# Two residual norms moved behind the products that follow them, and first projections started on six of eight feature tiles

## The chip, the cores and the metric

The kernel runs on one core of one Trainium2 chip. The metric is the device time of one execution in microseconds (us). The core has five engines that run side by side and meet only through semaphores: TensorE (PE, matrix products and transposes), VectorE (DVE), ScalarE (ACT), GpSimd (POOL) and SyncE (SP, which here only starts the weight DMAs).

## The reference, cut to what matters

256 tokens with 1024 features run through one first block and two layers of a second model; all is float32. The change touches the second half of the first block:

```python
merged = gate_a * (ya @ w_proj_a[i]) + gate_b * (yb @ w_proj_b[i])
h = h + merged @ w_out[i]
h = h + memory_cross_attention(rms_norm(h, xattn_norm_g[i]), memn, w_q[i], w_k[i], w_v[i], w_xo[i])
h = h + swiglu(rms_norm(h, ffn_norm_g[i]), w_gate[i], w_up[i], w_down[i])
# rms_norm(x, g) = x * rsqrt(mean(x * x) + 1e-6) * g, one factor per token
# swiglu(n) = (silu(n @ w_gate) * (n @ w_up)) @ w_down
# attention: softmax(q k^T / 16) v, 4 heads of 256, 256 memory rows
```

Each of the two later layers has the form `merged @ w_out` too, followed by a layer norm. The last layer ends in a mixture of experts, which fills the second half of the run.

## The kernel before

**Tiles.** The residual `h` lies in SBUF with tokens on partitions, as two blocks of 128 tokens by 1024 features. A product needs its input with features on partitions, so normed values are transposed by TensorE against an identity (8 feature tiles of 128, called k 0 to 7). PSUM has 8 banks of 128 x 512. Work is cut into units, one bank each, in the order of `plan_units`; a unit's bank is its number modulo 8.

**Split products.** The large products work on pairs of fp32r tiles: a value is its fp32r copy ("high", made by ACT) plus the rest ("low", made by DVE as value minus high). One product is then three matmuls: high x high, high x low, low x high. A weight chunk (1 MB, 256 output columns for 8 feature tiles) is thus 48 matmuls of 256 columns: `split_b` with tokens as output partitions, `split_a` with features as output partitions.

**Weights.** SP streams chunks into a ring of 7 slots (L556 to L563). ACT makes the high copy (`wp_part`, L1386), DVE the rest (`wp_rest`, L1841), into two slots wp 0 and 1; chunk n may be copied only when the unit that used chunk n-2 is full. The FFN has three slots of its own (`wf_part` L1363, `wf_rest` L1860).

**Order of work around the change.** Every engine's program is an order written out by hand:
- PE waits for all four quarters of `merged` (`m_split`, L1013), makes units out 0 to 2 (one quarter of 256 features of the residual each) and then the last quarter as two half units `last_out` 0 and 1, one per token block.
- DVE adds each unit to `h` (`residual`, L1767). For each half unit `last_norm` (L1890) adds it, finishes the statistics, waits for ACT's square root, takes the reciprocal and writes the normed block `xn` (L1900).
- PE transposes a normed block as soon as it stands (`block_transposes`, L657); ACT copies the transposed values times the norm's gain to `xf_h` (L1402), DVE writes `xf_l` (L1880). When all of it stands, the four q units (L713) run.
- Attention over memory follows (4 heads), then units xo 0 to 2 and `last_xo` in the same manner as out, then the first block's FFN: 11 steps of gate (48 matmuls, L832), up (48) and down (24 of 512 columns, L845).
- Layers 0 and 1 start their own out product with the same wait for four quarters (L1089).

The square root lives in another activation table than exp and silu, so ACT loads it beforehand (`load_sqrt`, L1276).

Of the kernel before, what the change touches and what calls it, by code (L numbers as in the profile page):

```python
# [31 lines left out]
P = 128  # L32
# [105 lines left out]
def split_plan():  # L138

    out = [((("k8", "w_" + n, i)), (n, i) if n == "q" or i < 3 else ("last_" + n, TB - 1))  # L140
           for n in ("out", "q", "xo") for i in range(4)]
# [12 lines left out]
def plan_units():  # L154
# [25 lines left out]
    add("out", 3)  # L180
    add("last_out", TB)
    add("t_xattn", 4)
    add("q", 4)
    attention_units(u, "x", 4)
    add("xo", 3)
    add("last_xo", TB)
    add("t_ffn", 4)
# [14 lines left out]
    return u  # L202

# [47 lines left out]
def build(nc, a, out):  # L251
    with ExitStack() as ctx:
# [27 lines left out]
        rsum = sb("rsum", [P, 2, 2 * TB])  # L280
        esink = sb("esink", [P, 2, 2 * TB])
# [96 lines left out]

        z_t = view(big, 8192, 2048, "p (b d) -> p b d", b=TB)
# [35 lines left out]
        block_ready = sem("block_ready")  # L415
# [211 lines left out]
        def _(pe):  # L627
# [77 lines left out]
            def split_a(unit, chunk, tiles=(0, 1)):  # L705
# [4 lines left out]
                for j in tiles:  # L710
                    for k in range(KD):
                        for i, (w, x) in enumerate(((wh, xf_h), (wh, xf_l), (wl, xf_h))):
# [7 lines left out]
            def split_b_block(unit, chunk, b, at):  # L720

                wh, wl = split_chunk(chunk)
                for k in range(KD):
                    for i, (x, w) in enumerate(((xf_h, wh), (xf_h, wl), (xf_l, wh))):
# [14 lines left out]
            def last_split_b(name, chunk):  # L739

                for b in range(TB):
                    open_unit(pe, (name, b))
                    close_unit(split_b_block((name, b), chunk, b, 0), (name, b))
# [133 lines left out]
            def ffn(name, next_unit):  # L877
                f0 = ff0[name]
                all_banks_free(next_unit)
                for n, (part, s) in enumerate(FF_ORDER):  # L880
                    if part == "gate" and s >= 2:
# [131 lines left out]
            pe.wait_ge(m_split, 4)  # L1013
# [4 lines left out]
            for b in range(TB):  # L1018
# [10 lines left out]
            for i in range(3):  # L1029
                split_b(("xo", i), ("k8", "w_xo", i))  # L1030
            last_split_b("last_xo", ("k8", "w_xo", 3))
            for b in range(TB):
                pe.wait_ge(block_ready, TB + b + 1)
                block_transposes("t_ffn", xn, b)
            evacuated(pe, ("t_ffn", 3))
            ffn("ffn", UNIT_AT[("t_in0", 0)])

            for m in range(2):
# [50 lines left out]
                pe.wait_ge(m_split, 4 + 4 * (m + 1))  # L1089
                for i in range(3):  # L1090
# [168 lines left out]
        def _(act):  # L1259
# [47 lines left out]
            def attention(name, heads, dst_of):  # L1307
                g0 = head0[name]
                for i in range(heads + 2):
                    if i < heads:  # L1310
                        g = g0 + i
                        act.wait_ge(negm_ready, g + 1)
                        for b in range(TB):
                            last = nc.scalar.activation(prob[:, g % 2, b, :],
                                                        bank((name + "_s", i))[:, b * 256:(b + 1) * 256], ACT.Exp,
                                                        bias=negm[:, g % 2, b:b + 1], scale=XSCALE,
# [78 lines left out]
            def copy_xf_gain(u0, b, gain):  # L1395

                for half in range(2):
                    u = (u0, 2 * b + half)
                    take_unit(act, u)
                    for j in range(4):  # L1400
                        k = 4 * half + j
                        last = nc.scalar.activation(xf_h[:, k, b * P:(b + 1) * P], bank(u)[:, j * P:(j + 1) * P],  # L1402
                                                    ACT.Identity, scale=gains[:, gain, k:k + 1])
                    last.then_inc(xf_high, 1)
# [7 lines left out]
            def ffn(name):  # L1412
                f0 = ff0[name]
                for n, (part, s) in enumerate(FF_ORDER):
                    if part == "gate":
                        act.wait_ge(g_full, f0 + s + 1)
                        if s >= 1:
                            act.wait_ge(hT_ready, f0 + s)
                        nc.scalar.activation(silu[:, :], psum[:, ff_bank(name, 2 * (s % 2)), :],
                                             ACT.Silu).then_inc(silu_ready, 1)  # L1420
# [98 lines left out]
            for _ in range(3):  # L1519
                wp_part()  # L1520
            load_sqrt()
            for b in range(TB):
                std_block(b)
            for b in range(TB):
                copy_xf_gain("t_xattn", b, 2)
            wp_part()
            for i in range(4):
                if i < 3:
                    wp_part()
                out_of(("q", i), qT[:, 2 * i:2 * i + 2, :], ACT.Copy)  # L1530
            attention("x", 4, lambda i: xf_h[:, 2 * i:2 * i + 2, :])
            for _ in range(3):
                wp_part()
            for n in range(SPLITS - 1):
                wf_part("ffn", n)
            load_sqrt()
            for b in range(TB):
                std_block(b)
            for b in range(TB):
                copy_xf_gain("t_ffn", b, 3)  # L1540
            wf_part("ffn", SPLITS - 1)
            ffn("ffn")
# [141 lines left out]
        def _(dve):  # L1684
# [11 lines left out]
            def stats(src, rms, eps, meanwhile=None):  # L1696
# [3 lines left out]
                for b in range(TB):  # L1700
                    for c in range(2):
# [71 lines left out]
            def attention(name, heads):  # L1773
                g0 = head0[name]
                for i in range(heads + 2):
                    if i < heads:
# [4 lines left out]
                        V.tensor_scalar(negm[:, g % 2, 0:TB], mx[:, g % 2, 0:TB], -XSCALE, None,  # L1781
# [12 lines left out]
                    if i >= 2:  # L1794
                        xf_rest_of((name + "_o", i - 2), "x_o", i - 2)
# [53 lines left out]
            def xf_rest_of(unit, use, i):  # L1849
# [3 lines left out]
                high = xf_h[:, 2 * i:2 * i + 2, :].bitcast(F32)  # L1853
                free_unit(V.tensor_tensor(xf_l[:, 2 * i:2 * i + 2, :], halves(bank(unit)), high, ALU.subtract), unit)
# [16 lines left out]
            def xf_rest_gain(u0, b, gain):  # L1871

                for half in range(2):
                    u = (u0, 2 * b + half)
                    take_unit(dve, u)
                    dve.wait_ge(xf_high, 4 * XF_USES.index(u0) + 2 * b + half + 1)
                    for j in range(4):
                        k = 4 * half + j
                        at = slice(b * P, (b + 1) * P)
                        last = V.scalar_tensor_tensor(xf_l[:, k, at], bank(u)[:, j * P:(j + 1) * P],  # L1880
                                                      gains[:, gain, k:k + 1], xf_h[:, k, at].bitcast(F32),
                                                      ALU.mult, ALU.subtract)
                    free_unit(last, u)

            def first_half_stats():

                for b in range(TB):
                    V.bn_stats(st[:, b, 0, :], h[:, b, 0:512])

            def last_norm(name, u0, gain):  # L1890

                for b in range(TB):
                    u = (name, b)
                    take_unit(dve, u)
                    hs = h[:, b, 768:1024]
                    free_unit(V.tensor_tensor(hs, hs, bank(u)[:, 0:256], ALU.add), u)
                    evacuated(dve, u)
                    block_stats(h, b, True, EPS, (1,))
                    block_rstd(b)
                    V.tensor_scalar(xn[:, b, :], h[:, b, :], rstd[:, b:b + 1], None, ALU.mult).then_inc(block_ready, 1)  # L1900
                for b in range(TB):
                    xf_rest_gain(u0, b, gain)

            def ffn(name):
                f0 = ff0[name]
                for n, (part, s) in enumerate(FF_ORDER):
                    if part == "up":
# [13 lines left out]
            def add_sums(name, n, b, alpha=None):  # L1921

                dve.wait_ge(down_done, FF_STEPS * n - (TB - 1) + b)
                for c in range(2):
                    hs = h[:, b, c * 512:(c + 1) * 512]
                    acc = psum[:, acc_bank(name, b, c), :]
                    if alpha is None:
                        last = V.tensor_tensor(hs, hs, acc, ALU.add)
# [192 lines left out]
            for i in range(3):  # L2121
                if i < 2:
                    wp_rest()
                residual(("out", i), i)
                if i == 1:
                    evacuated(dve, ("out", 1))
                    first_half_stats()
            wp_rest()
            evacuated(dve, ("out", 2))
            last_norm("last_out", "t_xattn", 2)  # L2130
            for _ in range(4):
# [385 lines left out]
```

## Time and profile before

| | |
|---|---|
| times of three runs | 2264.4, 2268.22, 2270.58 us (median 2268.22) |
| profiled execution | 2270.2 us, span of its records 2268.4 us |
| PE busy | 2144.6 us, 95% |
| DVE, ACT busy | 1577.0 us (70%), 1196.4 us (53%) |
| mean granted TensorE clock | 0.971 of 2.4 GHz |

The span is the time from the first to the last instruction. Lines such as L725 are lines of the kernel before; a line can be a helper's that several stages share, so stages are told apart by time. The out product runs from 296 to 321 us, q from 330 to 355, attention to 384, xo to 411, and the first FFN from 420 to 602 us.

### The profile page before, as it was taken

What the parts mean: (1) busy time and instruction counts of PE and PEld (TensorE: products, weight loads), DVE (VectorE), ACT (ScalarE), POOL (GpSimd) and SP (SyncE); (2) the same over time, 40 slices, a digit from 0 to 9 for tenths busy, and PEclk for the clock granted to TensorE, in tenths of its full rate; (3) what the DMA queues carried; (4) which work ended last, traced back from release to release, by engine and by line L of the source; (5) the groups of instructions that cost most, each with busy time, mean ns of one, the idle gap of its engine ahead of it and who ended that gap; (6) DMA issues with size and microseconds to landing.
All of it is one profiled execution on the core that took longest, in us unless ns stands there. A gap on an engine that the chain in (4) does not pass through costs nothing.

```text
span 2268.4 us, 33197 instructions
## 1 busy us (share of the span) xinstructions
PE 2144.6 (95%) x12590; PEld 1876.3 (83%) x12590; DVE 1577.0 (70%) x1775; ACT 1196.4 (53%) x1233; POOL 9.8 (0%) x22
## 2 busy tenths in 40 slices
PE   7999988899898989998888999999999999999997
PEld 7888877899797779998877788888888888888885
DVE  8677353544636454454555888989898989899897
ACT  3300233433337433343552677777777777777774
POOL 0000000000000000000000000000000000000000
PEclk9999998899999989999998899999999999999998
DMA  7343332355463235555323798989898989989894
GB/s 300 138 151 112 145 121 87 136 186 185 160 244 109 97 138 185 186 197 192 142 78 129 276 371 344 364 350 367 339 366 342 365 352 361 371 337 370 349 357 162
DMA packets 76446, 542.02 MB, mean 239 GB/s; under 512 B 9152, under 2 KB 9296, under 8 KB 11968
## 3 DMA queue, kind: packets, MB, share of 16 engines
q1 hardware_dynamic: 72144, 524.32, 60.3%
q0 software_dynamic: 2080, 10.40, 1.2%
q10 hardware_dynamic: 2128, 5.93, 0.7%
q8 instruction: 73, 1.20, 0.2%
q14 instruction: 21, 0.17, 0.0%
HBM read 539.57 MB, written 1.05 MB: 238 GB/s over the span
## 4 chain that ended last, share of the span: by engine, by line
PE 88%; DVE 6%; ACT 4%; issue 2%; DMA 0%; DVEq 0%; ACTq 0%
PE psum L1192 13%; PE psum L832 11%; PE psum L1169 9%; PE psum L1173 9%; PE psum L1172 9%; PE psum L666 7%; PE psum L713 6%; PE psum L725 6%; PE psum L845 4%; PE psum L679 3%; PE psum L692 3%; PE psum L1135 2%; PE psum L1181 1%; ACT wp_h L1386 1%; PE psum L989 1%
## 5 line engine op out<-in xcount | busy, mean ns | idle before, releaser
L2247 DVE TENSOR_TENSOR w_l<-ring,w_h 128x2048 fp32r<-128x2048 f32 x338 | 773.5, 2291 | 116.1 <-ACT w_h L1372 109.4
L1372 ACT ACTIVATE w_h<-ring 128x2048 fp32r<-128x2048 f32 x338 | 647.5, 1916 | 140.4 <-PE psum L1169 96.8
L1169 PE MATMUL psum<-w_h,xe_h 128*128 128x512 f32 x896 | 359.9, 402 | 2.4 <-DVE xe_l L2331 2.4
L1173 PE MATMUL psum<-w_h,xe_l 128*128 128x512 f32 x896 | 350.8, 391 | 0.0
L1172 PE MATMUL psum<-w_l,xe_h 128*128 128x512 f32 x896 | 350.2, 391 | 0.0
L1860 DVE TENSOR_TENSOR wf_l<-ring,wf_h 128x2048 fp32r<-128x2048 f32 x66 | 151.2, 2291 | 156.2 <-ACT wf_h L1363 156.2
L1841 DVE TENSOR_TENSOR wp_l<-ring,wp_h 128x2048 fp32r<-128x2048 f32 x52 | 119.1, 2292 | 163.5 <-ACT wp_h L1386 163.5
L832 PE MATMUL psum<-xf_h,wf_h 128*128 128x256 f32 x704 | 201.6, 286 | 4.7 <-DVE xf_l L1880 3.0
L832 PE MATMUL psum<-xf_l,wf_h 128*128 128x256 f32 x704 | 201.3, 286 | 0.0
L832 PE MATMUL psum<-xf_h,wf_l 128*128 128x256 f32 x704 | 201.3, 286 | 0.0
L1169 PEld LDWEIGHTS psum<-w_h,xe_h 128*128 128x128 f32 x896 | 168.8, 188 | 38.3 <-DVE w_l L2247 4.0
L1173 PEld LDWEIGHTS psum<-w_h,xe_l 128*128 128x128 f32 x896 | 168.6, 188 | 36.1
L1172 PEld LDWEIGHTS psum<-w_l,xe_h 128*128 128x128 f32 x896 | 169.1, 189 | 32.3
L1363 ACT ACTIVATE wf_h<-ring 128x2048 fp32r<-128x2048 f32 x66 | 126.0, 1912 | 114.0 <-PE psum L845 58.5
L1386 ACT ACTIVATE wp_h<-ring 128x2048 fp32r<-128x2048 f32 x52 | 99.5, 1916 | 141.4 <-PE psum L725 72.8
L832 PEld LDWEIGHTS psum<-xf_h,wf_h 128*128 128x128 f32 x704 | 137.5, 195 | 6.2 <-DVE xf_l L1880 3.4
L1192 PE MATMUL psum<-w_h,eT_h 128*128 128x512 f32 x448 | 140.0, 394 | 0.0
L1192 PE MATMUL psum<-w_h,eT_l 128*128 128x512 f32 x448 | 138.4, 390 | 0.0
L1192 PE MATMUL psum<-w_l,eT_h 128*128 128x512 f32 x448 | 138.3, 390 | 0.0
L725 PE MATMUL psum<-wp_h,xf_h 128*128 128x256 f32 x384 | 113.4, 295 | 26.0 <-DVE xf_l L1868 13.1
L832 PEld LDWEIGHTS psum<-xf_l,wf_h 128*128 128x128 f32 x704 | 137.3, 195 | 0.7
L832 PEld LDWEIGHTS psum<-xf_h,wf_l 128*128 128x128 f32 x704 | 137.3, 195 | 0.0
(370 smaller groups left out, 3721.0 us busy)
## 6 DMA issues: line engine op xcount, KB each, us to landing
ring<-in_stream SPq DMA_DIRECT2D x499, 1024.0 KB, 5.6
big<-in_bc POOLq DMA_DIRECT2D x11, 512.0 KB, 7.7
big<-in_na_bias POOLq DMA_DIRECT2D x2, 2048.0 KB, 9.6
h<-in_x SPq DMA_DIRECT2D x2, 512.0 KB, 4.3
big<-in_mem ACTq DMA_DIRECT2D x1, 1024.0 KB, 12.1
big<-in_s_c ACTq DMA_DIRECT2D x1, 1024.0 KB, 12.8
r_k<-in_sgu_ln ACTq DMA_DIRECT2D x1, 1024.0 KB, 18.0
out_dram<-ysum ACTq DMA_DIRECT2D x1, 1024.0 KB, 4.0
```

Of the source, the lines that this page charges most:

```text
L666: last = nc.tensor.matmul(bank(unit)[:, j * TOK:(j + 1) * TOK], w[:, k, j * P:(j + 1) * P], act_T[:, k, :], start=(k == 0), stop=(k == KD ...
L713: last = nc.tensor.matmul(bank(unit)[:, j * TOK:(j + 1) * TOK], w[:, k, j * P:(j + 1) * P], x[:, k, :], start=(k == i == 0), stop=(k == KD ...
L725: last = nc.tensor.matmul(bank(unit)[:, at * 256:(at + 1) * 256], x[:, k, b * P:(b + 1) * P], w[:, k, :], start=(k == i == 0), stop=(k == ...
L832: last = nc.tensor.matmul(psum[:, ff_bank(name, b), j * TOK:(j + 1) * TOK], w[:, k, j * P:(j + 1) * P], x[:, k, :], start=(k == i == 0), s ...
L1169: first = nc.tensor.matmul(out, xe_h[:, k, :], wh[:, i, :], start=(k == 0), stop=False)
L1172: nc.tensor.matmul(out, xe_h[:, k, :], wl[:, i, :], start=False, stop=False)
L1173: last = nc.tensor.matmul(out, xe_l[:, k, :], wh[:, i, :], start=False, stop=(k == KD - 1))
L1192: last = nc.tensor.matmul(psum[:, 4 + c, :], x[:, s % 2, k, :], w[:, k, c * 512:(c + 1) * 512], start=(s == 0 and k == n == 0), stop=(s == ...
L1363: nc.scalar.activation(wf_h[:, n % SPLITS, :], ring[:, at % SLOTS, :], ACT.Copy).then_inc(wf_high, 1)
L1372: nc.scalar.activation(high, src, ACT.Copy).then_inc(w_high, 1)
L1860: V.tensor_tensor(wf_l[:, n % SPLITS, :], ring[:, at % SLOTS, :], wf_h[:, n % SPLITS, :].bitcast(F32), ALU.subtract).then_inc(wf_split, 1)
L2247: V.tensor_tensor(low, src, high.bitcast(F32), ALU.subtract).then_inc(w_split, 1)
```

## The change

1. **Turned quarters.** The last quarter is an ordinary unit (out 3, xo 3). As soon as quarter i-1 of the residual stands, PE transposes the raw residual (no norm applied) between the two token blocks of unit i (`turn` in `turned_b`). ACT copies it times the gain to the high tile, DVE makes the rest. For the q stage these tiles and the attention's output are in the FFN's third weight slot (`xq_h`, `xq_l`), no longer in `xf_h`, `xf_l`.
2. **The norm's factor behind the products.** The factor is one number per token. For q it goes into the softmax's scale: exp reads `q_scale` instead of a constant, the maximum is multiplied with it. For the FFN, up is left raw, and the factor is applied to gate in DVE ahead of each silu (11 new multiplies of 128 x 512, which read a row of factors `rrow` made by two new matmuls and a copy) and once to the sum of the down products in `add_sums`.
3. **First chunks on six of eight tiles.** `first_a` (q 0, gate 0) runs feature tiles 0 to 5 for both halves and only then waits for the last quarter; the transposes of that quarter stand between the halves. `first_b` (out 0, and out 0 of both layers) does the same with three quarters of `merged`.
4. `last_norm`, `xn` in these two places, `block_transposes` of it, and the per block square roots there are gone; one square root over both blocks remains.

```diff
-            for i in range(3):
-                split_b(("out", i), ("k8", "w_out", i))
-            last_split_b("last_out", ("k8", "w_out", 3))
-            for b in range(TB):
-                pe.wait_ge(block_ready, b + 1)
-                block_transposes("t_xattn", xn, b)
-            evacuated(pe, ("t_xattn", 3))
-            for i in range(4):
-                split_a(("q", i), ("k8", "w_q", i))
+            first_b(("out", 0), ("k8", "w_out", 0), 0)
+            turned_b("out", "t_xattn", xf_h, xf_l)
+            evacuated(pe, ("t_xattn", 2))
+            open_unit(pe, ("q", 0))
+            close_unit(first_a(bank(("q", 0)), split_chunk(("k8", "w_q", 0)), xq_h, xq_l, "t_xattn", "out", ...), ("q", 0))
+            for i in range(1, 4):
+                split_a(("q", i), ("k8", "w_q", i), x_h=xq_h, x_l=xq_l)
...
+            def turned_b(name, turned, x_h, x_l):
+                for i in range(1 if name == "out" else 0, 4):
+                    open_unit(pe, (name, i))
+                    for b in range(TB):
+                        last = split_b_block((name, i), ("k8", "w_" + name, i), b, b, x_h, x_l)
+                        if b == 0 and i >= 1:
+                            turn((turned, i - 1), name)
+                    close_unit(last, (name, i))
+            def first_a(out, w_parts, x_h, x_l, turned, added, used):
+                wh, wl = w_parts
+                for ks in (range(0, 6), range(6, KD)):
+                    if ks[0] == 6:
+                        evacuated(pe, (turned, 3))
+                    for j in range(2):
+                        for k in ks:
...
+                        if ks[0] == 0 and j == 0:
+                            turn((turned, 3), added)
+            def first_b(unit, chunk, split0):
+                pe.wait_ge(m_split, split0 + 3)
...
+                    if ks[0] == 6:
+                        pe.wait_ge(m_split, split0 + 4)
```
ACT and DVE of the out and q stage, and DVE of the FFN's entry (the xo stage is like out):
```diff
+            for u in range(3):
+                wp_part()
+                copy_turned(("t_xattn", u), xq_h, 2)
+            wp_part()
+            load_sqrt()
+            copy_turned(("t_xattn", 3), xq_h, 2)
+            for i in range(4):
+                if i < 3: wp_part()
+                if i == 0: std()
+                out_of(("q", i), ...)
...
+            for i in range(3):
+                residual(("out", i), i)
+                wp_rest()
+                xf_rest_of(("t_xattn", i), "t_xattn", i, xq_h, xq_l, 2)
+                if i >= 1: first_half_stats(i - 1)
+            residual(("out", 3), 3)
+            xf_rest_of(("t_xattn", 3), "t_xattn", 3, xq_h, xq_l, 2)
+            wp_rest()
+            stats(h, True, EPS, parts=(1,))
...
+            residual(("xo", 3), 3)
+            stats(h, True, EPS, parts=(1,))
+            for b in range(TB):
+                last = V.tensor_scalar(rwide[:, b, :], ones[:, :], rstd[:, b:b + 1], None, ALU.mult)
+            xf_rest_of(("t_ffn", 3), "t_ffn", 3, xf_h, xf_l, 3)
+            wf_rest("ffn", 2)
+            link(V.tensor_copy(rrow, psum[:, acc_bank("ffn", 0, 0), 0:TOK]))
```

## Rows read from the trace of the kernel before

**Rows 1.** The page, part 1: busy us (share of the span), instructions.
```profile
PE 2144.6 (95%) x12590; PEld 1876.3 (83%) x12590; DVE 1577.0 (70%) x1775; ACT 1196.4 (53%) x1233; POOL 9.8 (0%) x22
```
**Rows 2.** Chain of waits, 295 to 355 us: start, us, engine, tile, line.
```profile
295.86 19.01 PE psum L725 x144
...
321.54 0.75 DVE r_gb L1900
...
329.82 24.84 PE psum L713 x192
...
354.69 0.60 ACT r_zu L1305
```
**Rows 3.** Chain of waits, 383 to 445 us.
```profile
383.62 11.79 PE psum L725 x96
...
403.88 4.55 PE psum L725 x24
...
419.55 25.88 PE psum L832 x192
```
**Rows 4.** Waits of PE, 290 to 440 us: total, times, longest us.
```profile
PE psum L713 <- DVE xf_l L1880: 3.3, 1, 3.3
PE psum L832 <- DVE xf_l L1880: 3.0, 1, 3.0
PE psum L725 <- DVE xf_l L1846: 2.9, 1, 2.9
PE psum L725 <- DVE wp_l L1841: 2.7, 1, 2.7
```
**Rows 5.** Windows: PE, PEld, DVE, ACT, POOL busy (instructions), granted clock, DMA.
```profile
799.00:800.00 1.00, 1.00 (x6) 1.00 (x6) 0.00 (x0) 0.00 (x0) 0.00 (x0) 0.50 0.98 418
801.00:802.00 1.00, 1.00 (x11) 1.00 (x10) 0.00 (x0) 0.00 (x0) 0.00 (x0) 1.00 0.03 8
1206.00:1207.00 1.00, 1.00 (x11) 1.00 (x10) 0.00 (x0) 0.00 (x0) 0.00 (x0) 1.00 0.00 0
```
**Rows 6.** Chain of waits, 52 to 57 us: transposes against the identity.
```profile
53.30 3.49 PE psum L910 x32
```
**Rows 7.** Timeline of ACT: start, us, line, operation, tiles, forms, count, idle before.
```profile
38.27 1.56 ACT L1299 ACTIVATE memT<-psum,gains 128x256 f32<-128x256 f32 x4
...
303.43 1.92 ACT L1386 ACTIVATE wp_h<-ring 128x2048 fp32r<-128x2048 f32 x1 [8.35 <-PE psum L725]
...
316.89 1.28 ACT L1276 ACT_TABLE_LOAD   x1
318.18 0.20 ACT L1276 ACTIVATE warm<-ones 128x1 f32<-128x1 f32 x1
...
358.30 0.47 ACT L1314 ACTIVATE r_zv<-psum,negm 128x256 f32<-128x256 f32 x1 [1.71 <-DVE negm L1781]
```
**Rows 8.** Timeline of DVE, 294 to 435 us, same columns.
```profile
294.33 1.47 DVE L1846 TENSOR_TENSOR xf_l<-r_ga,xf_h 128x512 fp32r<-128x512 f32 x2
...
305.38 2.29 DVE L1841 TENSOR_TENSOR wp_l<-ring,wp_h 128x2048 fp32r<-128x2048 f32 x1 [9.57 <-ACT wp_h L1386]
307.59 0.68 DVE L1767 TENSOR_TENSOR h<-h,psum 128x512 f32<-128x512 f32 x1
...
314.06 1.29 DVE L1888 BATCH_NORM_STATS2 st<-h 128x6 f32<-128x512 f32 x2
...
319.11 0.41 DVE L1896 TENSOR_TENSOR h<-h,psum 128x256 f32<-128x256 f32 x1
...
320.29 0.21 DVE L1723 BATCH_NORM_AGGREGATE mv<-st 128x2 f32<-128x12 f32 x1
...
389.67 0.69 DVE L1767 TENSOR_TENSOR h<-h,psum 128x512 f32<-128x512 f32 x1 [2.77 <-PE psum L725]
...
434.02 0.69 DVE L1910 TENSOR_TENSOR silu<-silu,psum 128x512 f32<-128x512 f32 x1 [1.11 <-PE psum L832]
```
**Rows 9.** Timeline of ACT in one FFN step: the silu of a gate.
```profile
541.59 0.60 ACT L1419 ACTIVATE silu<-psum 128x512 f32<-128x512 f32 x1 [3.66 <-PE psum L832]
```
**Rows 10.** Timeline of DVE in the same step.
```profile
544.02 2.29 DVE L1860 TENSOR_TENSOR wf_l<-ring,wf_h 128x2048 fp32r<-128x2048 f32 x1 [3.77 <-ACT wf_h L1363]
```
**Rows 11.** Chain of waits from 430 us: down products, next gate and up.
```profile
547.31 5.47 PE psum L845 x24
552.78 11.51 PE psum L832 x96
```

More of the change, by code:

```diff
@@ L179, in plan_units @@
     add("pa", 4)
[L180 to L183, printed above, removed]
+    turned_units(u, "out", "t_xattn")
+    u += [("q", 0), ("t_xattn", 3)]
+    u += [("q", i) for i in range(1, 4)]
     attention_units(u, "x", 4)
-    add("xo", 3)
-    add("last_xo", TB)
-    add("t_ffn", 4)
+    turned_units(u, "xo", "t_ffn")
+    u.append(("t_ffn", 3))
     for m in range(2):
@@ new lines, in first_b @@
+            def first_b(unit, chunk, split0):
+                pe.wait_ge(m_split, split0 + 3)
+                open_unit(pe, unit)
+                wh, wl = split_chunk(chunk)
+                for ks in (range(0, 6), range(6, KD)):
+                    if ks[0] == 6:
+                        pe.wait_ge(m_split, split0 + 4)
+                    for b in range(TB):
+                        for k in ks:
+                            for i, (x, w) in enumerate(((xf_h, wh), (xf_h, wl), (xf_l, wh))):
+                                last = nc.tensor.matmul(bank(unit)[:, b * 256:(b + 1) * 256],
+                                                        x[:, k, b * P:(b + 1) * P], w[:, k, :],
+                                                        start=(b == k == i == 0), stop=(k == KD - 1 and i == 2),
+                                                        skip_group_check=True)
+                                if i == b == k == 0:
+                                    release(last, chunk)
+                close_unit(last, unit)
@@ L1393, in merged_high, with copy_turned @@
                                          ).then_inc(xf_high, 1)
[L1395 to L1404, printed above, removed]
+            def copy_turned(unit, dst, gain):
+                take_unit(act, unit)
+                for j in range(2):
+                    k = 2 * unit[1] + j
+                    last = nc.scalar.activation(dst[:, k, :], bank(unit)[:, j * TOK:(j + 1) * TOK], ACT.Identity,
+                                                scale=gains[:, gain, k:k + 1])
+                last.then_inc(xf_high, 1)
             def copy_xf_block(u0, b):
@@ L1869, in xf_rest_block, with ffn @@
                                               quarter(xf_h, u).bitcast(F32), ALU.subtract), (u0, u))
[L1871 to L1904, printed above, removed]
+            def ffn(name, raw=False):
                 f0 = ff0[name]
                 for n, (part, s) in enumerate(FF_ORDER):
+                    if part == "gate" and raw:
+                        dve.wait_ge(g_full, f0 + s + 1)
+                        if s >= 1:
+                            dve.wait_ge(hT_ready, f0 + s)
+                        row = rrow.unsqueeze(1).to_broadcast([P, 2, TOK])
+                        V.tensor_tensor(halves(silu[:, :]), halves(psum[:, ff_bank(name, 2 * (s % 2)), :]), row,
+                                        ALU.mult).then_inc(gate_scaled, 1)
                     if part == "up":
@@ L2122, in _ @@
+            V.tensor_scalar(q_scale[:, 0, :], rstd[:, :], XSCALE, None, ALU.mult)
+            link(V.tensor_scalar(q_scale[:, 1, :], rstd[:, :], -XSCALE, None, ALU.mult))
+            for _ in range(3):
+                wp_rest()
+            attention("x", 4)
+            wp_rest()
+            wf_rest("ffn", 0)
+            for i in range(3):
+                residual(("xo", i), i)
                 if i < 2:
                     wp_rest()
[L2124 to L2127, printed above, removed]
```

184 lines of the change are left out of this document (109 added, 75 removed).

## The prediction, made before the changed kernel was run

> **What bounds the kernel now.** I read the busy shares first. PE is busy 95% of the span [rows 1], so only PE's idle time (124 us), its time at half clock, and products could be saved. Next the chain of waits: in the stages the change touches it leaves PE at four places. Ahead of out it is on DVE (`xf_l` of `merged`); between out and q it runs DVE, ACT, DVE through the norm, from the end of out to 329.82 [rows 2]; inside xo DVE's weight rest comes late, and after xo the norm comes again, up to 419.55 [rows 3]. The table of PE's waits puts sizes on their last links: 2.9, 3.3, 2.7 and 3.0 us [rows 4]; the rest of each norm gap is shorter waits around the transposes.
>
> Each gap costs twice. The window at 799 us shows a granted clock of 0.50 (1.2 GHz) with 6 matmuls in a us, the one at 801 us 1.00 (2.4 GHz) with 11 [rows 5]. That slow stretch began 1 us after a 2.9 us idle time of PE. 48 matmuls at full clock take 5.76 us (11.51 for 96 [rows 11]); q took 24.84 us for 192 instead of 23.04 [rows 2], so 1.8 us went to the slow clock and small waits.
>
> **How I sum.** I take two intervals between events that both kernels have, so that gaps, slow matmuls and hidden work are all inside, and add the three early starts. Time zero of each interval is the end of its first unit.
>
> **Part A, out 0's end to q 3's end.** Before: ACT's weight copy that waits for out 0 starts at 303.43 [rows 7], ACT's copy of q 3 at 354.69 [rows 2]: 51.3 us.
> After, PE first: out 1 to 3 are 3 x 5.76 plus 3 x 4 transposes. 32 transposes take 3.49 us [rows 6], 0.109 each, so 0.44 per turn: 18.6 us. This holds only if DVE keeps up, and each unit (6.2 us) holds on DVE: residual 0.68, then a wait for ACT's 1.92 us weight copy (which waits for the unit itself, so until 2.0), weight rest to 4.3 (2.29), turned rest to 5.15 (two of 128x256, put at 0.42 each from the 0.41 us of L1896), half statistics to 5.8 (1.29 for two) [rows 7, 8]. It fits with 0.4 us to spare; before, this stretch of out was covered in the same way.
> Then q 0, counted from out 3's end. PE: 18 matmuls, turn, 18 matmuls = 4.76. ACT in its order: weight copy to 2.0, table load and dummy root 1.48, to 3.45, turned copy (4 of 128x256 in 1.56 [rows 7], with its tail 0.86 for two) to 4.3. DVE then needs 0.85, to 5.2. So PE stalls about 0.5 us, and ends q 0 at 6.7. The weight rest for q 1 stands behind the turned rest on DVE: 5.2 to 7.5, so PE stalls 0.8 more. q 1 ends at 13.25. The weight rest for q 2 stands behind the norm: statistics from 7.5 (1.3, two aggregates 0.4, three small operations 0.6), root, reciprocal and the two factors to 10.7, rest to 13.0: 0.25 us early. The single root on ACT and its wait delay only the copy of q 0. q 3 ends at 24.8. Sum 18.6 + 24.8 = 43.4; saved 7.9 us.
>
> **Part B, xo 0's end to up 0's end.** Before: 389.67 to 434.02 [rows 8], 44.35 us; in it are the late weight rest, the norm gap and the longest slow stretch (the first 192 FFN matmuls took 25.88 us instead of 23.04 [rows 3]). After: 18.6 for xo 1 to 3; the FFN's first weight chunk is now prepared ahead of xo 0's residual (ACT is free about a us ahead of xo 0's start at 383.62 [rows 3]; two copies of 1.92, the second with its 2.29 rest behind the first's, end near 389.2, just in time), and the second sits where xo 2's wp rest was, so the late rest is gone. From xo 3's end: DVE residual and statistics to 3.15, root to 3.4; ACT copies the turned quarter only after that root, to 4.3; DVE reciprocal, two wide rows (0.5), turned rest to 5.15. PE is at 4.76 and stalls 0.45. Gate 0 ends at 6.65, the two factor matmuls (0.2), up 0 at 12.8. Sum 31.4; saved 12.95 us.
>
> **Part C, first_b, three times.** The wait falls from the fourth quarter to the third; two rests take 1.47 us [rows 8], so PE starts 0.72 us earlier, and the last quarter is ready behind 36 matmuls (4.3 us). In layers 0 and 1 the chain after it starts at a unit's end, so it moves whole. 3 x 0.72 = 2.15 us.
>
> **What is added elsewhere.** 11 gate multiplies on DVE at about 0.7 us (the 0.69 of L1910 [rows 8]) stand ahead of silu and of the weight rest. In a step the silu starts at 541.59, the weight rest behind it ends at 546.31, and its chunk is needed at 552.78 [rows 9 to 11]: 6.5 us of cover, so zero. If that cover were gone each step would pay 0.7, 7 us in all. At the entry the first multiply stands behind the weight rest and the factor copy, silu ends at about 10.1, ahead of 12.8. `add_sums` keeps its size (0.68 against 0.68, nothing). No row shows exp with a factor read from a tile beside its bias; from below it costs nothing, from above half of the small root's whole length of 0.20 us [rows 7], 0.1 each on an exp of 0.47; eight of them, half hidden: I take 0.3 us, ends 0 and 0.8.
> The Trainium skill, "ScalarE: Activation LUTs", section "What ACT_TABLE_LOAD costs", says that each pointer operand adds about 93 ns; that would be 0.7 us if nothing hid it, 0.4 us off the sum. No run here shows it yet.
> On the turns rows and rule differ in use. The row gives 0.109 us from start to start, with a length of 0.27 each that overlaps. The Trainium skill, "TensorE: Matmul & The Clock Gate", section "Part 4: PE-mode transpose", gives some 275 ns for a transpose in a kernel; if turns paid that in full inside the products, 32 of them would cost 8.8 us instead of 3.5, and the gain would be 5.3 us smaller. I go by the row.
>
> **Sum.** 7.9 + 12.95 + 2.15 - 0.3 = 22.7 us. The profiled execution would go from 2270.2 to 2247.5; the median of the runs lies 2.0 below it, so I predict 2245.5 us, -1.0%. What is late next in both stages is the last turned quarter (ACT's table load and root ahead of its copy) and q 1's weight rest on DVE.
>
> **Rivals.**
> - R1, DVE and ACT become the bound of the turned stages. For: only 0.4 us to spare per unit, 0.25 at q 2. Against: the durations are steady. If each of six turned units and q 1 to q 3 slipped by 0.5, 4.5 us: 2250.
> - R2, the clock. The new stalls (0.5, 0.8, 0.45) may bring a slow stretch, 15 matmuls at 0.213 instead of 0.12, 1.4 us, or 27 at gate 0, 2.5; both: 2249.4. For: a drop came after a 2.7 us wait. Against: PE ran at full clock through the 2.9 us gap before 1206 [rows 5]. The other way, the two slow stretches behind the out gaps vanish as these shrink to 2.2 us: 2242.7.
> - R3, it doesn't do what it says: the last quarter's chain is as long as the norm was, and q 0 and gate 0 wait for it with both halves done. The norm's chain from the last half unit to the first matmul was 9.2 us at out (329.82, less the 320.6 that 48 matmuls behind the first 144 reach [rows 2]); here 5.2 is forecast behind 4.8 of cover. If it took 9.2, each stage lost 4 more: 2253.5.
> - R4, slower. The gate multiply on DVE lengthens multiply, silu, weight copy, weight rest until the next chunk is late in every step. It decides only beyond 6.5 us of added delay [rows 9 to 11]; to turn the sign it has to cost 2.1 us in each of 11 steps, thus 8.6 us of delay against 0.7 that the rows show. At 2.5 us a step: 2273.
>
> **How the numbers follow.** Forecast as summed 63% (own range 2243 to 2248), R1 11%, R2 15% (both ways), R3 8%, R4 3%. The range takes in R1, R2 and the unknown exp: 2240.5 to 2251. About 0.3% (7 us) can be told from no change here. Faster by more than that: all but R4 and a little of R3, 95%; within 2%, slower 3%.
>
> **What would show it.** PE: no idle time above 1 us from out 0 to q 3 and from xo 0 to up 0; stalls near 0.5 inside q 0 and gate 0, 0.8 ahead of q 1. Granted clock 1.00 from out 1 to q 3. The two intervals at 43.4 and 31.4 us. FFN steps still 16.98 us apart (5.47 + 11.51), multiplies near 0.7 us. Waits for `merged` at 2.2 instead of 2.9. Wrong would be: turned copies or rests ending after their unit, a step longer than 17 us, or a clock of 0.5 inside q or gate 0.

## The result and the profile after

The changed kernel took 2245.52 us (median of 5, 2242.58 to 2247.36), the kernel before beside it 2268.22 us (median of 5, 2257.37 to 2271.35). The ratio of the runs is 0.9915, with a 95% interval of 0.9894 to 0.9936: 14 to 24 us less. The forecast was 2245.5 us and 22.7 us less, the range 2240.5 to 2251. Later runs of the same kernel before, 33 on another chip, had a median of 2261.76, so a part of the hit is luck, and the sections below say which.

The page after, part 1 (columns as in [rows 1]):
```profile
PE 2136.8 (95%) x12594; PEld 1869.5 (83%) x12594; DVE 1583.0 (71%) x1761; ACT 1196.3 (53%) x1215; POOL 9.8 (0%) x22
```
PE is busy 7.8 us less although it has 4 more matmuls and 4 more weight loads: that is half-clock time saved (not all of it by the change, as the second traces below show). The span fell by 24.7 us to 2243.7, so 17 us came from PE's idle time.

The chain of waits after, between out and q; it answers to [rows 2]. The second fence is its later part, from the second half of gate 0 over up 0, gate 1 and up 1 to down 0, and answers to [rows 3]:
```profile
295.78 7.52 PE psum L803 x48
303.30 2.88 PE psum L739 x24
306.18 0.44 PE psum L760 x4
...
318.99 2.88 PE psum L739 x24
...
321.95 1.92 ACT wp_h L1456
...
323.89 1.28 ACT L1346
...
326.24 0.88 DVE wf_l L1933 x2
327.12 2.21 DVE wp_l L1915
...
329.46 17.52 PE psum L727 x144
...
347.00 0.61 ACT r_zu L1375
```
```profile
403.71 1.70 PE psum L783 x12
405.41 0.45 PE psum L954 x4
405.86 17.27 PE psum L898 x144
423.12 2.07 PE psum L911 x9
```
L803 is `first_b`, L760 a turn, L739 the other products of out (and xo), L727 q, L783 the FFN's first chunk (`first_a`), L954 the factor's matmuls, L898 gate and up, L911 down. Products run from 295.78 to 321.87 with only turns between them. The chain then goes over ACT's weight copy and table load to the turned rest and to q 1's weight rest, which lets q 1 start.

PE's waits after, 290 to 430 us; they answer to [rows 4]:
```profile
PE psum L803 <- DVE xf_l L1920: 2.1, 1, 2.1
...
PE psum L727 <- DVE wp_l L1915: 0.6, 1, 0.6
PE psum L783 <- DVE wf_l L1933: 0.6, 1, 0.6
PE psum L783 <- DVE xf_l L1933: 0.2, 1, 0.2
```
The wait for `merged` is 2.1 instead of 2.9 us. `first_a` (L783) waits 0.6 us inside q 0 and 0.2 inside gate 0; ahead of q 1 the wait is 0.6. The granted clock was 1.00 from 304 to 347 us and from 380.3 to 423 us, so no slow stretch lies in q or in the FFN's entry any more.

**Where the time went, by stage.** Each border is an event that both kernels have: the start of an ACT copy that waits for a unit or, at down 0 and behind each layer's first part, the end of the products ahead of it; for both kernels I have two traces. "Again" is the second, told below.

| stage, us | before | before again | after | after again |
|---|---|---|---|---|
| start to out 0's end | 303.4 | 301.8 | 303.4 | 303.6 |
| A: out 0's end to q 3's end | 51.3 | 51.6 | 43.6 | 43.6 |
| attention and xo 0 | 35.0 | 33.4 | 33.3 | 31.6 |
| B: xo 0's end to down 0 | 55.7 | 54.9 | 42.8 | 42.8 |
| rest of the FFN, norm, first part of layer 0 | 207.5 | 207.1 | 208.7 | 208.5 |
| layer 0 to its out 0's end | 151.0 | 145.2 | 145.4 | 145.4 |
| to the dense FFN's down 0 | 55.3 | 54.6 | 55.2 | 55.1 |
| dense FFN, first part of layer 1 | 204.1 | 205.2 | 205.4 | 205.3 |
| layer 1 to its out 0's end | 148.4 | 146.2 | 148.4 | 148.4 |
| to the end | 1056.8 | 1056.8 | 1057.6 | 1058.2 |

The borders of A and B after:
```profile
303.40 1.92 ACT L1456 ACTIVATE wp_h<-ring 128x2048 fp32r<-128x2048 f32 x1 [7.61 <-PE psum L803]
...
380.29 1.92 ACT L1456 ACTIVATE wp_h<-ring 128x2048 fp32r<-128x2048 f32 x1 [3.33 <-PE psum L739]
```
They end at 347.00 (ACT's copy of q 3) and 423.12 (down 0). In the kernel before A repeats within 0.3 us and B within 0.8; after the change both repeat within 0.1. So A saved 7.7 to 8.0 and B 12.1 to 12.9 us. The other rows move by up to 6 us between two executions of one kernel.

### The profile page after: what moved, and what is told of

Read it like the earlier page. It is cut to its first block, busy times and chain, and to the rows that moved or that the text cites. A ratio compares the mean times of both kernels' runs of the same rounds, so it can differ in the third digit from the quotient of the medians.

```text
span 2243.7 us, 33172 instructions
## 1 busy us (share of the span) xinstructions
PE 2136.8 (95%) x12594; PEld 1869.5 (83%) x12594; DVE 1583.0 (71%) x1761; ACT 1196.3 (53%) x1215; POOL 9.8 (0%) x22
## 4 chain that ended last, share of the span: by engine, by line
PE 89%; DVE 5%; ACT 4%; issue 1%; DMA 0%; DVEq 0%; ACTq 0%
PE psum L1262 13%; PE psum L898 11%; PE psum L1239 9%; PE psum L1243 9%; PE psum L1242 9%; PE psum L680 7%; PE psum L739 6%; PE psum L727 5%; PE psum L911 4%; PE psum L693 3%; PE psum L706 3%; PE psum L1205 2%; PE psum L1251 1%; PE psum L803 1%; ACT wp_h L1456 1%
## 5 line engine op out<-in xcount | busy, mean ns | idle before, releaser
L898 PE MATMUL psum<-xf_h,wf_h 128*128 128x256 f32 x688 | 195.6, 284 | 1.9 <-DVE xf_l L1952 1.9
L898 PE MATMUL psum<-xf_l,wf_h 128*128 128x256 f32 x688 | 195.5, 284 | 0.0
L898 PE MATMUL psum<-xf_h,wf_l 128*128 128x256 f32 x688 | 195.4, 284 | 0.0
L898 PEld LDWEIGHTS psum<-xf_h,wf_h 128*128 128x128 f32 x688 | 132.9, 193 | 3.0 <-DVE xf_l L1952 2.3
L898 PEld LDWEIGHTS psum<-xf_l,wf_h 128*128 128x128 f32 x688 | 132.8, 193 | 0.7
L898 PEld LDWEIGHTS psum<-xf_h,wf_l 128*128 128x128 f32 x688 | 132.8, 193 | 0.0
L727 PE MATMUL psum<-xf_h,wp_h 128*128 128x256 f32 x384 | 110.0, 286 | 0.0
## 6 DMA issues: line engine op xcount, KB each, us to landing
big<-in_mem ACTq DMA_DIRECT2D x1, 1024.0 KB, 12.1
big<-in_s_c ACTq DMA_DIRECT2D x1, 1024.0 KB, 12.9
r_k<-in_sgu_ln ACTq DMA_DIRECT2D x1, 1024.0 KB, 17.5
```

The lines of the kernel that those rows point to most:

```text
L898: last = nc.tensor.matmul(psum[:, ff_bank(name, b), j * TOK:(j + 1) * TOK], w[:, k, j * P:(j + 1) * P], x[:, k, :], start=(k == i == 0), s ...
```

## The experiments

### The same kernels again
No edit. Before:


> The kernel before, unchanged, for a second trace. My theory, that the slow clock stretches behind idle times of PE fall differently in each execution: the same waits of PE (2.9 ahead of out, norm gaps 9.2 and 11.1 us), but other places of the slow stretches; attention over memory and in the layers may differ by 1 to 3 us. Rival: the stretches lie at the same places (then a shift of the schedule moved them, and the gain of 5 us in the two attentions belongs to the change).


After:


> The kernel after, unchanged, for a second trace. Same theory: intervals 43.6 and 31.5 us again, attention intervals and the layers' norms different from the first trace by 1 to 3 us. Rival: all stages repeat within 0.3 us.


One run each: 2258.48 and 2244.33 us. The cores' views (span, mean granted clock) of before, before again, after, after again:
```profile
core 0: 2268.4 us, clock 0.971
```
```profile
core 0: 2256.7 us, clock 0.977
```
```profile
core 0: 2243.7 us, clock 0.975
```
```profile
core 0: 2242.5 us, clock 0.978
```
At a mean clock of 0.971 PE was granted half its speed for 2 x 0.029 x 2268 = 132 us, at 0.977 for 104. 28 us more at half speed cost up to 14 us; the spans differ by 11.7. Half of that lies in layer 0, where the windows (columns as in [rows 5]) show it; first before, then before again:
```profile
655.00:796.30 141.30, 125.86 (x889) 113.21 (x887) 76.23 (x101) 74.79 (x146) 0.00 (x0) 0.96 0.33 119
```
```profile
651.00:787.00 136.00, 121.19 (x888) 109.22 (x887) 75.37 (x100) 74.56 (x146) 0.00 (x0) 1.00 0.34 123
```
The same matmuls but for one at the border, PE busy 4.7 us longer at 0.96. So my theory held for the kernel before; for the kernel after only attention over memory moved (1.7 us), and the layers repeated to 0.1 us. The 5.6 us of layer 0 between the first traces are not the change's.

The times tell the same: of the kernel before's 33 executions that stood beside the next four kernels 22 took 2256.8 to 2262.2 us and 11 took 2266.5 to 2272.7, none between. The trace I had predicted from is one of the upper group.

### One stage alone
`out_only` takes xo and the FFN's entry back, `xo_only` takes out and q back. Core of the edits to the kernel after:
```diff
-            turned_b("xo", "t_ffn", xq_h, xq_l)
-            evacuated(pe, ("t_ffn", 2))
-            ffn("ffn", UNIT_AT[("t_in0", 0)], True)
+            for i in range(3):
+                split_b(("xo", i), ("k8", "w_xo", i), xq_h, xq_l)
+            last_split_b("last_xo", ("k8", "w_xo", 3), xq_h, xq_l)
+            for b in range(TB):
+                pe.wait_ge(block_ready, b + 1)
+                block_transposes("t_ffn", xn2, b)
+            evacuated(pe, ("t_ffn", 3))
+            ffn("ffn", UNIT_AT[("t_in0", 0)])
```


> The out and q stage and all first_b starts as after the change, xo and the FFN's entry as before it (its own norm, no factor behind the products; the normed block lies in another tile). My theory, that the gain is the sum of stages that don't know of each other: out 0's end to q 3's end 43.6 us as after the change, xo 0's end to up 0's end 44.4 us as before it; the time is 2268.2 - 7.7 - 2.2 = 2258.3 us. Rival (the stages share the gain: a norm gap left in xo takes back what out gave, or the clock does): the second interval grows by more than 2 us, or the time is above 2263.


```diff
-            turned_b("out", "t_xattn", xf_h, xf_l)
...
-            for i in range(1, 4):
-                split_a(("q", i), ("k8", "w_q", i), x_h=xq_h, x_l=xq_l)
+            for i in range(1, 3):
+                split_b(("out", i), ("k8", "w_out", i))
+            last_split_b("last_out", ("k8", "w_out", 3))
+            for b in range(TB):
+                pe.wait_ge(block_ready, b + 1)
+                block_transposes("t_xattn", xn, b)
+            evacuated(pe, ("t_xattn", 3))
+            for i in range(4):
+                split_a(("q", i), ("k8", "w_q", i))
```


> The out and q stage as before the change except first_b, xo and the FFN's entry with the raw residual as after it (the norm for q is applied ahead of q, exp with a constant scale). My theory: out 0's end to q 3's end 51.3 us, xo 0's end to up 0's end on PE 31.5, FFN steps 16.98 us; the time is 2268.2 - 12.9 - 2.2 = 2253.1 us. Rival (the gate multiply costs in the steps): steps longer than 17.1 us, time above 2256.

Measured: `out_only` 2254.62 us (ratio 0.9962, 0.9947 to 0.9977), `xo_only` 2253.52 (0.9955, 0.9937 to 0.9973), both beside 2261.76. Intervals: A 43.6 and B 55.6 in `out_only`, A 52.1 and B 42.8 in `xo_only`. Each stage gives its own part whatever the other does, which is what the first theory says; the gains of the two ratios add to 0.83%, beside 0.85% for the whole change. The absolute figures are no support for my sums. `out_only`'s 2254.62 is 3.7 us below mine, which started from 2268.2; from 2261.8 it would be 2251.9, and the kernel is 2.7 above. `xo_only`'s 2253.52 meets my 2253.1 by luck: from 2261.8 the same sum gives 2246.7, 6.8 too low. What was missing is in the traces, as the sections below show: the early starts gain only in layer 0 (0.8 us), and the changed xo and FFN cost 1.2 us in the rest of the FFN and 0.9 in layer 0. With these the stages add up to 8.5 us for `out_only`, 11.6 for `xo_only` and 19.3 for the whole change; the ratios, of 2262 us, give 8.6, 10.2 and 19.2, each uncertain by 3 to 5. FFN steps are 16.98 us in both.

Attention and xo 0 take 33.26 us in `out_only`, whose exp reads its factor from a tile, and 33.25 in `xo_only`, whose exp has a constant. The exp itself, in timelines of ACT, `xo_only` and after:
```profile
358.20 0.47 ACT L1393 ACTIVATE r_zv<-psum,negm 128x256 f32<-128x256 f32 x1 [1.71 <-DVE negm L1875]
```
```profile
350.61 0.56 ACT L1384 ACTIVATE r_zv<-psum,negm,q_scale 128x256 f32<-128x256 f32 x1 [1.71 <-DVE negm L1855]
```
The second operand costs 0.09 us, and none of it reached PE. The Trainium skill, "ScalarE: Activation LUTs", section "What ACT_TABLE_LOAD costs", gives about 93 ns; the row agrees.

### The early starts alone
```diff
-            pe.wait_ge(m_split, 4)
-            for i in range(3):
+            first_b(("out", 0), ("k8", "w_out", 0), 0)
+            for i in range(1, 3):
                 split_b(("out", i), ("k8", "w_out", i))
```
and the same in both layers, on the kernel before.


> The kernel before with first_b alone, at all three out products. My theory: PE's waits for merged fall from 2.9 to 2.1 us each and nothing else moves; 2268.2 - 2.2 = 2266.0 us. Rival (the clock): the shorter gaps stop the slow stretches behind them, 1.4 us more for each that goes: 2263. Rival (nothing): 2268.


Measured 2262.71 beside 2261.76, ratio 0.9992 (0.9975 to 1.001): no difference that can be told. The three waits are 2.1 us, as expected, but its 12 runs lie closer together (10 of them 2260.8 to 2266.2, the others 2258.5 and 2269.1) than the two groups of the kernel before.

### Without the early starts
```diff
             def first_b(unit, chunk, split0):
-                pe.wait_ge(m_split, split0 + 3)
+                pe.wait_ge(m_split, split0 + 4)
```
on the kernel after.


> The kernel after with the three out products waiting for all four quarters of merged again. First theory (part C is worth its 0.72 us three times): waits 2.9 us, time 2245.0 + 2.2 = 2247.2. Rival, from the traces so far (where the wait ahead of layer 1's out is 2.1 us its 48 first matmuls took 7.6 us in 6 of 7 traces, where it is 2.9 they took 6.1 in 2 of 3): the clock takes back what the early start gives, 2245 to 2246, and the place of the slow stretches changes.


Measured 2248.8 (6 runs), ratio 0.9930 (0.9911 to 0.9950). The runs fall in two groups again, 2240.4 and 2243.1, and 2248.2 to 2250.7; the trace is of the fastest one, span 2238.5, which is 4 to 5 us shorter than either trace of the kernel after. First matmul of layer 1's out in timelines of PE, after and without the early starts:
```profile
1178.48 0.39 PE L803 MATMUL psum<-wp_h,xf_h 128*128 128x256 f32 x1 [2.11 <-DVE xf_l L1920]
```
```profile
1175.51 0.39 PE L803 MATMUL psum<-wp_h,xf_h 128*128 128x256 f32 x1 [2.90 <-DVE xf_l L1920]
```
and the ends of that unit (ACT's copy that waits for it):
```profile
1186.07 1.92 ACT L1456 ACTIVATE wp_h<-ring 128x2048 fp32r<-128x2048 f32 x1 [7.58 <-PE psum L803]
```
```profile
1181.63 1.92 ACT L1456 ACTIVATE wp_h<-ring 128x2048 fp32r<-128x2048 f32 x1 [6.90 <-PE psum L803]
```
The same 48 matmuls take 7.6 us behind the shorter wait and 6.1 behind the longer one. The first block's out 0 did the opposite in the same trace: 8.8 us behind 2.9, where both traces of the kernel after have 7.6 behind 2.1. Inside the slower unit, windows of the kernel after:
```profile
1179.00:1180.00 1.00, 1.00 (x10) 1.00 (x10) 0.21 (x1) 0.00 (x0) 0.00 (x0) 0.95 0.00 0
1181.00:1182.00 1.00, 1.00 (x6) 1.00 (x6) 0.00 (x0) 0.00 (x0) 0.00 (x0) 0.50 1.01 426
```
It starts at 2.4 GHz and falls to 1.2 on the way. Over all 13 traces layer 1's first unit was slow in 8 of the 9 with a 2.1 us wait, and in 1 of the 4 with 2.9. In layer 0 it was the other way: fast in all 9 traces with 2.1, slow in 2 of 4 with 2.9. In the first block it was slow in 8 of 9 with 2.1 and in 3 of 4 with 2.9. So what an early start gives, 0.8 us, is less than the 1.5 us that a slow stretch takes. That the early start brings the slow stretch in layer 1 is the rival's reading and fits, but isn't shown: `xo_only` had the 2.1 us wait too and ran fast.

In layer 0 the 0.8 us do arrive: its interval is 146.2 us here and 145.4 in the kernel after, 145.2 in before again and 144.4 in `first_b_only`. The kernel after has them and loses 0.9 elsewhere in that layer. In the layer's attention, behind an idle time of PE of 3.0 us in every trace, the clock falls in all nine traces with the factor behind the FFN's products and in none of the four without it. Windows of after, then before again:
```profile
681.88:683.88 2.00, 1.94 (x10) 1.73 (x12) 0.31 (x1) 1.26 (x1) 0.00 (x0) 0.50 0.03 8
```
```profile
698.92:700.92 2.00, 1.94 (x17) 1.64 (x17) 1.04 (x3) 1.26 (x1) 0.00 (x0) 1.00 0.04 8
```
The code there is unchanged, and why it falls isn't known.

What the early starts are worth in the mean stays open: the median says 3.3 us for them, the spans of the traces 4 to 5 us against them, and the two ratios overlap. My first figure, 2247.2, is nearer to the median of 2248.8 than the rival's 2245 to 2246.

### A shift of the whole schedule
```diff
                 dve.wait_ge(loads[f"x{b}"], 16)
+                if b == 1:
+                    for _ in range(2):
+                        link(V.bn_stats(st[:, 1, 0, :], h[:, 1, 0:512]))
```


> The kernel after with two more half statistics (2 x 0.72 us) on DVE ahead of the first normed block, so that all that follows starts 1.4 us later. Theory (the clock's slow stretches follow the time passed since something outside the schedule): they fall at other places of the schedule than in both traces of the kernel after, and the time differs from 2245 + 1.4 by 1 to 5 us. Rival (they follow the schedule itself): the same stages slow, 2246.4.


Measured 2247.28 (4 runs, 2244.76 to 2250.73), ratio 0.9931 (0.9908 to 0.9954). Against the traces of the kernel after one of the three units changed (out 0 ran fast, 6.1 instead of 7.6 us), layer 0's and layer 1's did not. The time is 0.9 us above the rival's 2246.4, just short of the 1 to 5 us of the theory. Inconclusive between the two.

### All eight tiles first
```diff
                 wh, wl = w_parts
+                turn((turned, 3), added)
+                evacuated(pe, (turned, 3))
                 for ks in (range(0, 6), range(6, KD)):
-                    if ks[0] == 6:
-                        evacuated(pe, (turned, 3))
...
-                        if ks[0] == 0 and j == 0:
-                            turn((turned, 3), added)
...
-                pe.wait_ge(m_split, split0 + 3)
+                pe.wait_ge(m_split, split0 + 4)
```
with the unit t_xattn 3 ahead of q 0.


> The kernel after with the first chunks waiting for all eight feature tiles: q 0 and gate 0 turn the last quarter first and wait for it, the out products wait for all four quarters. My theory: PE idles about 4 us ahead of q 0 and of gate 0 (weight copy, table load, copy, rest: 5.2 us from out 3's end, 5.15 from xo 3's), q 3 ends 3.4 us later, up 0 4.3 us later, the three out starts 0.75 each: 2245.5 + 9.9 = 2255.4, and with a slow clock stretch behind each of the two idle times up to 4 more, 2259. Rival (the six of eight start is hidden by the weights anyway, q 1's rest being late): under 2250.


Measured 2260.65, ratio 0.9982 (0.9967 to 0.9997), 15 us above the kernel after. PE's waits, 290 to 440 us:
```profile
PE psum L783 <- DVE wf_l L1931: 3.7, 1, 3.7
PE psum L783 <- DVE xf_l L1931: 3.3, 1, 3.3
PE psum L801 <- DVE xf_l L1918: 2.9, 1, 2.9
PE psum L760 <- DVE h L1839: 2.0, 2, 1.0
```
A is 49.7 (6.1 more), B 49.4 (6.6 more): waits of 4.7 and 4.3 us (the turn's 1.0 included) plus slower matmuls behind them; the whole is 1.7 us above the upper end of what I had written (2259). With the raw residual turned and the factor behind the products, but the starts on all tiles, 4 us are left of the gain of 19. The two traces are 17.5 us apart, and 12.7 of them lie in A and B; 3.9 lie in layer 0 and 0.8 in layer 1, where the wait was 2.9 us again and the clock fell behind it. The turn moves the norm out of the chain; the 36 matmuls on six tiles cover what remains of the chain (weight copy, table load, copy, rest). A kernel with the six-tile start but the norm still ahead of the products was not run, so how much of A and B the turn and the factor give by themselves is read from this run alone.

### The cover of the gate multiply
Four more multiplies in steps 1 to 9 (`gate5`), and nine more (`gate10`):
```diff
+                        for _ in range(5 - 1 if 0 < s < FF_STEPS - 1 else 0):
+                            link(V.tensor_tensor(halves(silu[:, :]), ... row, ALU.mult))
                         V.tensor_tensor(halves(silu[:, :]), ... row, ALU.mult).then_inc(gate_scaled, 1)
```


> The kernel after with the gate multiply done 5 times instead of once in steps 1 to 9 of the first FFN (4 x 0.72 = 2.9 us more on DVE ahead of each silu and weight rest). My theory (6.5 us of cover, of which the one multiply uses 0.7): steps stay at 16.98 us, no difference. Rival (the multiply's delay reaches the down products or the next chunk): 9 steps x up to 2.9 = up to 26 us slower.

> The same with 10 multiplies in steps 1 to 9 (9 x 0.72 = 6.5 us more ahead of each silu). My theory: the weight rest behind them ends 12.0 us after the gate's end, its chunk is due at 11.2, so each step pays 0.8 us or somewhat more, 7 to 18 us in all. Rival (the cover is larger than I count, since nothing else waits): no difference.


Measured: five multiplies 2244.97 (4 runs, ratio 0.9906), steps 16.98 us, and one new wait of 0.4 us at the last down product. Ten: 2258.65 (ratio 0.9971, 0.9958 to 0.9984), 13.7 above. Its chain of waits:
```profile
426.21 2.30 DVE wf_l L1944
428.65 6.00 PE psum L898 x48
...
442.45 1.92 ACT wf_h L1433
444.39 2.31 DVE wf_l L1944
446.83 6.00 PE psum L898 x48
```
A step takes 18.18 us instead of 16.98, and the chain goes over ACT's weight copy and the rest behind the silu, the place that R4 named. Nine steps make 10.9 us; the other 2.8 are one wait of PE at the last down product (`hf_l`). The cover is real and ends about where it was read: 2.9 us more cost nothing in the steps, 6.5 us more cost 1.2 a step.

### The late links moved
```diff
+            copy_turned(("t_xattn", 3), xq_h, 2)
             load_sqrt()
-            copy_turned(("t_xattn", 3), xq_h, 2)
...
+            copy_turned(("t_ffn", 3), xf_h, 3)
             std()
-            copy_turned(("t_ffn", 3), xf_h, 3)
...
+            wp_rest()
             xf_rest_of(("t_xattn", 3), "t_xattn", 3, xq_h, xq_l, 2)
-            wp_rest()
...
-            stats(h, True, EPS, parts=(1,))
+            stats(h, True, EPS, lambda: xf_rest_of(("t_ffn", 3), "t_ffn", 3, xf_h, xf_l, 3), parts=(1,))
...
-            xf_rest_of(("t_ffn", 3), "t_ffn", 3, xf_h, xf_l, 3)
```


> The kernel after with the two late links moved: ACT copies the last turned quarter ahead of the table load (q) and ahead of the root (FFN); DVE makes q 1's weight rest ahead of the turned rest, and the FFN's last turned rest ahead of the reciprocal. My theory: the 0.6 us wait ahead of q 1 goes, the 0.2 us one in gate 0 goes, the one in q 0 stays near 0.5; interval A 43.0, B 31.4 on PE (down 0 at 42.6 from xo 0's end); 0.8 us less, 2244.2, too little for the timing to tell, so the intervals decide. Rival (the norm becomes late behind the moved work): a new wait ahead of q 2 or of up 0.


Measured 2242.32 (6 runs, 2240.12 to 2245.1), ratio 0.9906 (0.9888 to 0.9924). PE's waits, 290 to 430 us:
```profile
PE psum L803 <- DVE xf_l L1920: 2.1, 1, 2.1
...
PE psum L783 <- DVE wf_l L1933: 0.5, 1, 0.5
```
The waits ahead of q 1 and in gate 0 are gone, no new one came. A is 42.7 (0.9 less), B 42.4 (0.4 less). This version is the shortest measured here by its intervals; its 3 us against the kernel after are within what two medians can differ.

## Why the prediction was right, and where it was not

**Part A** (43.4 forecast) measured 43.6. Out 1 to 3 with their turns took 18.6 as summed; q 0's wait was 0.6 (0.5 forecast), q 1's 0.6 (0.8), q 2 came without one. DVE kept up with 0.4 us to spare, its idle time ahead of the residual of out 2, so R1 did not happen:
```profile
315.70 0.69 DVE L1841 TENSOR_TENSOR h<-h,psum 128x512 f32<-128x512 f32 x1 [0.45 <-PE psum L739]
```
R2's slow stretches behind the new stalls did not come either: the granted clock was 1.00 in both intervals.

**Part B** (55.7 less 12.95, 42.75) measured 42.83 (up 0's end 31.5 behind xo 0's, where 31.4 was forecast); the wait in gate 0 was 0.2, not 0.45. The turned copy on ACT started 0.1 us behind the start of the 0.20 us root (401.86 and 401.75), which I had put one behind the other. Against the second trace of before it saved 12.1: that trace had 0.8 us less to lose. R3 is excluded by the waits: the last quarter's chain took 5.2 us at out (321.95 to 327.12), as forecast. `wait_all` shows what a chain without cover costs.

**Turns.** The chain has 0.44 us for 4, with products right behind them: the row from the start of the kernel held inside the products, and none of the 5.3 us was lost that the gain would have shrunk by with the length of one transpose in the Trainium skill, "TensorE: Matmul & The Clock Gate", section "Part 4: PE-mode transpose".

**Part C** (2.15 us). The waits fell by 0.79 us each, a little more than forecast, but the step that in layers 0 and 1 the chain behind "moves whole" failed: in layer 1 the unit behind the shorter wait ran slow (48 matmuls in 7.6 us), 1.5 us back, and its interval is 148.4 in both first traces. Between the first traces the start of the kernel up to out 0's end has 303.4 both times too. I had priced the clock only in the favourable sense at these places (the slow stretch behind the first block's gap did not vanish), and `first_b_only` measured no gain. Of the 2.15 us only layer 0's 0.8 is to be found in the traces.

**What is added elsewhere** (0.3 us, in exp). Exp cost nothing that the intervals show. The FFN did: its stage takes 207.1 to 207.5 us in the four traces with the norm ahead of it and 208.5 to 208.9 in the seven with the factor behind its products (`gate5` and `gate10` aside), also in `xo_only`. In the second-last step two weight chunks of the next stage are prepared as well, so the cover that I read from a step in the middle is used up there. Timeline of DVE, after again:
```profile
565.12 2.29 DVE L1944 TENSOR_TENSOR wf_l<-ring,wf_h 128x2048 fp32r<-128x2048 f32 x1 [0.56 <-ACT wf_h L1433]
567.33 2.28 DVE L1915 TENSOR_TENSOR wp_l<-ring,wp_h 128x2048 fp32r<-128x2048 f32 x1
569.53 0.68 DVE L1963 TENSOR_TENSOR silu<-psum,big 128x512 f32<-128x512 f32 x1
572.72 2.29 DVE L1944 TENSOR_TENSOR wf_l<-ring,wf_h 128x2048 fp32r<-128x2048 f32 x1 [2.50 <-ACT wf_h L1433]
574.93 0.68 DVE L1968 TENSOR_TENSOR silu<-silu,psum 128x512 f32<-128x512 f32 x1
...
581.84 1.40 DVE L1986 SCALAR_TENSOR_TENSOR h<-psum,rstd,h 128x512 f32<-128x512 f32 x2
```
The last multiply (L1963) waits for nothing but DVE itself, the last product (L1968) follows a weight rest without idle time, where it had waited 1.11 us for PE before, and comes 0.35 us later in the stage; `add_sums` takes 1.40 for two, where before again had 1.28. That is 0.6 us with its second block. The remaining 0.8 is the clock in the first products of layer 0 (8.3 us for 48 matmuls, 7.5 in before again). That difference, too, divides the traces: in every one with the factor behind the products these 48 are slower than in every one without it. Whether it follows from the 0.6 wasn't tested. The 0.9 us in layer 0's attention come on top, so a term put at 0.3 us was about 2. These traces differ in the turned xo as well as in the factor, and only the 0.6 us are traced to the added DVE work.

**The whole.** Between the first traces A gave 7.7 us, B 12.9 and the FFN's stage -1.2, 19.4 in all; the span fell by 24.7, and the rest is mostly layer 0, 5.6 us of clock against a trace of the upper group. With the second traces the fall is 14.2. The timed ratio, 19 us at its centre, lies between. Direction, the mechanism of A and B and their sizes were right. Two smaller terms were wrong, and both made the sum too favourable: part C gave 0.8 us instead of 2.15, and what is added elsewhere cost about 2 instead of 0.3. That the absolute figure was hit all the same is luck: the starting time was one that 33 more runs put 6 us lower, and from 2261.8 the sum would have given 2239.1, outside my range and 6.4 us below what was measured.

## What to carry to other kernels

A norm whose factor is one number per token can go behind the products, but most of the gain comes from covering what is left of the chain: here, without the starts on part of the tiles, 15 of 19 us were lost, and by the traces 12.7 us of that in the two stages with a norm. Read the cover of an added operation in the step where the most else is scheduled, not in one from the middle. Before a sum from one trace is put against a median, take a second trace of the same kernel: stages of unchanged code differed by 6 us here.

## What the runs showed that I had not expected

- The kernel before has two groups of times, 22 and 11 of 33 executions with a gap of 4 us between them (in the other sets of executions three runs lie well inside it, 2264.4 twice and 2265.1), and the kernel after without the early starts has them too (2 and 4 of 6). The kernel after (5 runs), `xo_only` (10) and `out_only` (12) show one.
- A wait of 2.1 us was followed by a slow stretch in layer 1 in 8 of 9 traces and never in layer 0 (0 of 9), though the code ahead of both is written the same; 2.9 us was followed by one in 1 of 4 in layer 1 and in 2 of 4 in layer 0. The length of a wait alone doesn't say whether the clock falls. What does is open.
- A stretch of unchanged code, the attention of layer 0, kept its full clock behind an idle time of 3.0 us in the four traces with the norm ahead of the FFN and lost it behind the same 3.0 us in the other nine. The places follow the kernel as well as the execution.
